# The opening of a two-block transformer kernel: the first two tiles of x as transfers and splits of their own

## What is computed

```
D_MODEL = 1024; BATCH = 1; SEQ = 256
def first_block(x, p, norm_mix_pre, w_in, ...):
    h = rms_norm(x, norm_mix_pre[l])
    z = jnp.einsum('bsd,dn->bsn', h, w_in[l])
    zq, zf_f, zf_b, zi, zg, zu, zv, ga, gb = jnp.split(z, offsets, axis=-1)
    a_out = hgrn2_mixer(...)                 # recurrent mixer on zq, zf, zi, zg
    b_out = spatial_gating(zu, zv, ...)      # gMLP unit
    merged = sigmoid(ga) * (a_out @ w_a) + sigmoid(gb) * (b_out @ w_b)
    x = x + rms_norm(merged @ w_out, norm_mix_post[l])
    ...                                      # feed-forward and a gated addition of p
def second_block(...):                       # attention, feed-forward with relu squared
    ...
def reference(...):
    return second_block(first_block(x, ...), ...)
```

## Time and profile before

| | us |
|---|---|
| median of 3 runs (804.22 to 804.37) | 804.32 |
| span of the profiled execution | 804.2 |
| that execution's whole time | 805.98 |
| PE busy in the span | 797.6 (99%) |
| ACT, DVE, POOL busy | 465.2, 571.0, 109.4 |

### The profile page before, as it was taken

How to read it: one execution, slowest core, us unless ns; L and a number is a source line. 1 busy time by engine, 2 the same in 40 slices (tenths; PEclk the granted TensorE clock), 3 DMA queues, 4 the chain that set the end, 5 groups by cost and what they waited for, 6 DMA issues and landing times.

```text
span 804.2 us, 13648 instructions
## 1 busy us (share of the span) xinstructions
PE 797.6 (99%) x5836; PEld 700.6 (87%) x5836; DVE 571.0 (71%) x713; ACT 465.2 (58%) x614; POOL 109.4 (14%) x82
## 2 busy tenths in 40 slices
PE   8999999999999999999999999999999999999998
PEld 7999988888888898888888889988899888888886
DVE  5877896796576587666676688688978865656653
ACT  6679784665534575454454575387787644444442
POOL 0101691662100000000000010111610100000000
PEclk9999999999999999999999999999999999999999
DMA  8744444453554555555555555456423555555541
GB/s 307 284 171 172 159 158 158 143 172 112 204 176 151 218 184 180 209 174 192 205 170 200 198 170 206 168 211 162 137 89 110 199 180 187 209 175 192 210 156 53
DMA packets 37820, 143.03 MB, mean 178 GB/s; under 512 B 9426, under 2 KB 11490, under 8 KB 24320
## 3 DMA queue, kind: packets, MB, share of 16 engines
q1 hardware_dynamic: 36576, 138.69, 49.7%
q0 software_dynamic: 1040, 3.43, 1.3%
q10 hardware_dynamic: 144, 0.04, 0.0%
HBM read 141.08 MB, written 1.06 MB: 177 GB/s over the span
## 4 chain that ended last, share of the span: by engine, by line
PE 96%; ACT 2%; DMA 2%; DVE 1%; issue 0%; POOL 0%; SPq 0%
PE ps L2392 8%; PE ps L2385 7%; PE ps L2032 6%; PE ps L2284 6%; PE ps L2285 6%; PE ps L2286 6%; PE ps L1964 6%; PE ps L2038 6%; PE ps L2035 6%; PE ps L1965 6%; PE ps L1966 6%; PE ps L2390 4%; PE ps L2387 4%; DMA raw<-w 2%; PE ps L2140 1%; PE ps L2300 1%
## 5 line engine op out<-in xcount | busy, mean ns | idle before, releaser
L1182 DVE TENSOR_TENSOR wlo<-raw,whi 128x2048 fp32r<-128x2048 f32 (+2 forms) x128 | 289.4, 2263 | 76.3 <-ACT whi L626 74.9
L626 ACT ACTIVATE whi<-raw 128x2048 fp32r<-128x2048 f32 (+2 forms) x128 | 241.3, 1888 | 105.6 <-DMA raw<-w 105.6
L1964 PE MATMUL ps<-xx,whi 128*128 128x256 f32 x396 | 114.1, 288 | 0.0
L1965 PE MATMUL ps<-xx,whi 128*128 128x256 f32 x396 | 112.0, 283 | 0.0
L1966 PE MATMUL ps<-xx,wlo 128*128 128x256 f32 x396 | 112.0, 283 | 0.0
L2284 PE MATMUL ps<-whi,xx 128*128 128x512 f32 x216 | 84.1, 389 | 0.0
L2285 PE MATMUL ps<-whi,xx 128*128 128x512 f32 x216 | 84.0, 389 | 0.0
L2286 PE MATMUL ps<-wlo,xx 128*128 128x512 f32 x216 | 84.0, 389 | 0.0
L2032 PE MATMUL ps<-whi,xx 128*128 128x512 f32 x208 | 83.0, 399 | 0.0
L2038 PE MATMUL ps<-wlo,xx 128*128 128x512 f32 x208 | 81.1, 390 | 0.0
L2035 PE MATMUL ps<-whi,xx 128*128 128x512 f32 x208 | 81.0, 390 | 0.0
(11 more groups left out here) (324 smaller groups left out, 1367.6 us busy)
## 6 DMA issues: line engine op xcount, KB each, us to landing
raw<-w SPq DMA_DIRECT2D x105, 1024.0 KB, 4.8
raw<-w SPq DMA_DIRECT2D x42, 512.0 KB, 5.0
raw<-w SPq DMA_DIRECT2D x8, 256.0 KB, 6.3
x<-xT SPq DMA_DIRECT2D x4, 256.0 KB, 5.7
work<-bias_scratch POOLq DMA_DIRECT2D x1, 1024.0 KB, 7.8
raw<-w SPq DMA_DIRECT2D x4, 192.0 KB, 3.3
out<-x SPq DMA_DIRECT2D x3, 256.0 KB, 2.5
raw<-w SPq DMA_DIRECT2D x3, 240.0 KB, 3.3
```

What stands on the lines that cost most here:

```text
L626: A(hi, full, ACT.Copy).then_inc(sem("hi_ready"), 1)
L1182: V.tensor_tensor(lo, full, hi.bitcast(F32), ALU.subtract)\
L1964: mm(out, hi, xh[:, tile, :], start=start, stop=False, skip_group_check=skip)
L1965: mm(out, hi, xl[:, tile, :], start=False, stop=False, skip_group_check=skip)
```

## The change

The first pair of x tiles is taken apart. SP issues x tile 0 (128 KB, `x_in0`), piece 0, x tile 1 (128 KB, `x_tile1`), piece 1, and goes on as before. ACT and DVE split tile 0, piece 0, tile 1, piece 1, each tile with its own wait and its own signal, where the two tiles stood together ahead of the two pieces. So the stage `n1` has five signals `act_hi` and `act_lo` and not four, and the waits of PE and of `gained_lo` count accordingly. The semaphores `b_hi` and `p_hi` become one, `side_hi`, and `b_lo` and `p_lo` become `side_lo`; the second user waits for 2.

```diff
-    "hi": dict(n1=4, a=4, m=4, n3=4, ff=4, n5=4, c=4, n6=4),
-    "lo": dict(n1=4, a=4, m=4, n3=4, ff=4, n5=4, c=4, n6=4),
+    "hi": dict(n1=5, a=4, m=4, n3=4, ff=4, n5=4, c=4, n6=4),
+    "lo": dict(n1=5, a=4, m=4, n3=4, ff=4, n5=4, c=4, n6=4),
...
             for k, pieces in enumerate(PIECES):
-                sp.dma_start(x[:, 2 * k:2 * k + 2, :], xT[:, 2 * k:2 * k + 2, :]).then_inc(sem(f"x_in{k}"), 16)
+                if k:
+                    sp.dma_start(x[:, 2 * k:2 * k + 2, :], xT[:, 2 * k:2 * k + 2, :]).then_inc(sem(f"x_in{k}"), 16)
                 for i in pieces:
+                    if k == 0:
+                        sp.dma_start(x[:, i, :], xT[:, i, :]).then_inc(sem(("x_in0", "x_tile1")[i]), 16)
                     u, cols = first_piece(i)
...
-            pool.wait_ge(sem("p_lo"), 1)
+            pool.wait_ge(sem("side_lo"), 2)
...
             for k, pieces in enumerate(PIECES):
-                act.wait_ge(sem(f"x_in{k}"), 16)
-                gained_hi("n1", "mix_pre", 0, k)
+                if k:
+                    act.wait_ge(sem(f"x_in{k}"), 16)
+                    gained_hi("n1", "mix_pre", 0, k)
                 for i in pieces:
+                    if k == 0:
+                        act.wait_ge(sem(("x_in0", "x_tile1")[i]), 16)
+                        A(xh[:, i, :], x[:, i, :], ACT.Copy, scale=col("mix_pre", i)).then_inc(sem("act_hi"), 1)
                     first_hi(i)
...
-                dve.wait_ge(sem("act_hi"), before("hi", name) + k + 1)
+                dve.wait_ge(sem("act_hi"), before("hi", name) + k + (2 if name == "n1" else 1))
...
+            def first_x_lo(i):
+
+                dve.wait_ge(sem(("x_in0", "x_tile1")[i]), 16)
+                dve.wait_ge(sem("act_hi"), i + 1)
+                V.scalar_tensor_tensor(xl[:, i, :], x[:, i, :], col("mix_pre", i), xh[:, i, :].bitcast(F32), ALU.mult, ALU.subtract)\
+                    .then_inc(sem("act_lo"), 1)
...
-                pe.wait_ge(sem("act_hi"), i // 2 + 1)
+                arrivals = i // 2 + 2 if i else 1
+                pe.wait_ge(sem("act_hi"), arrivals)
...
-                pe.wait_ge(sem("act_lo"), i // 2 + 1)
+                pe.wait_ge(sem("act_lo"), arrivals)
```

More of the change, by code:

```diff
@@ L801, in _ @@
                     act.wait_ge(sem("b_out"), 1)
-                    A(xh[:, 16:20, :], bout, ACT.Copy).then_inc(sem("b_hi"), 1)
+                    A(xh[:, 16:20, :], bout, ACT.Copy).then_inc(sem("side_hi"), 1)
             heads_hi_turned(2)
@@ L830, in _ @@
             act.wait_ge(sem("p_in"), 16)
-            A(xh[:, 16:18, :], pT_s, ACT.Copy).then_inc(sem("p_hi"), 1)
+            A(xh[:, 16:18, :], pT_s, ACT.Copy).then_inc(sem("side_hi"), 1)
             ahead(U_WOUT)
@@ L1250, in first_sum @@
                 link(V.tensor_tensor(sq1[:, 0:2, :], sq1[:, 0:2, :], sq1[:, 2 * k:2 * k + 2, :], ALU.add))
+            def first_x_lo(i):
[3 more added lines that the diff above has]
+                    .then_inc(sem("act_lo"), 1)
             for k, pieces in enumerate(PIECES):
-                dve.wait_ge(sem(f"x_in{k}"), 16)
-                gained_lo("n1", "mix_pre", 0, k)
+                if k:
+                    dve.wait_ge(sem(f"x_in{k}"), 16)
+                    gained_lo("n1", "mix_pre", 0, k)
                 for i in pieces:
+                    if k == 0:
+                        first_x_lo(i)
                     first_lo(i)
@@ L1420, in _ @@
                 if u == 7:
-                    dve.wait_ge(sem("b_hi"), 1)
-                    V.tensor_tensor(xl[:, 16:20, :], bout, xh[:, 16:20, :].bitcast(F32), ALU.subtract).then_inc(sem("b_lo"), 1)
+                    dve.wait_ge(sem("side_hi"), 1)
+                    V.tensor_tensor(xl[:, 16:20, :], bout, xh[:, 16:20, :].bitcast(F32), ALU.subtract).then_inc(sem("side_lo"), 1)
             def merged_lo(j):
@@ L1486, in tile_residual @@
                                        x[:, m, :], ALU.mult, ALU.add).then_inc(sem(name + "_x"), 1)
-            dve.wait_ge(sem("p_hi"), 1)
-            V.tensor_tensor(xl[:, 16:18, :], pT_s, xh[:, 16:18, :].bitcast(F32), ALU.subtract).then_inc(sem("p_lo"), 1)
+            dve.wait_ge(sem("side_hi"), 2)
+            V.tensor_tensor(xl[:, 16:18, :], pT_s, xh[:, 16:18, :].bitcast(F32), ALU.subtract).then_inc(sem("side_lo"), 1)
             V.memset(rel_s[0:33, 0, 0:HEADS], 1.0).then_inc(sem("rel_one"), 1)
@@ L2246, in _ @@
             heads_turned(1)
-            pe.wait_ge(sem("b_lo"), 1)
+            pe.wait_ge(sem("side_lo"), 1)
             bank_free(U_WB, B_BANKS[0][0])
@@ L2342, in _ @@
             arrived(U_PLE)
-            pe.wait_ge(sem("p_lo"), 1)
+            pe.wait_ge(sem("side_lo"), 2)
             ple_part(range(3))
```

## The result

The changed kernel takes 806.13 us (median of 21 runs, 805.60 to 806.88) where the kernel before takes 804.46 us on the same chip (median of 21, 804.19 to 805.37): a ratio of 1.0017, 95% interval 1.0011 to 1.0023. It is slower by 1.7 us between the two medians and by 1.4 us by the ratio (1.0017 of 804.46), outside the predicted range of 803.6 to 805.3. A few executions of several kernels took far longer (867 to 4479 us) and are left out of every ratio.

The account below looks back on a forecast made before the run. The prediction took the opening to be bound by the landing of piece 5, with PE waiting 1.16 us. Start 0 plus landings 0.1 plus 0 made +0.1 on the median 804.32: 804.4 us, range 803.6 to 805.3.

Parts of the forecast that it names:

- The base: Whole kernel: took the profiled span of 804.2 as 0.1 below the median of 804.32, and added the change to that median.
- PE has 1.16 us of slack against it: Opening, PE ahead of piece 5: supply ends last (13.72), so a sooner start only lengthens PE's 1.16 us wait.
- The start: PE's first product: from 6.19 to about 5.8, 0.4 to 0.5 us won at 7.7, but worth 0.0 at the end.
- Rival D: Opening: piece 0 lands no earlier and the start stays at 6.1; same time as forecast, counted in its 0.52 chance.
- the gains at 4.56 are untouched: ACT's start on x: the gains still land at 4.56, so tile 0 can't start sooner, however early it lands.
- covered, by 0.3 us: Piece 1 in the opening: lands at 6.1 to 6.3, high part at about 6.9, PE wants it at 7.2.
- The landings, +0.1 (bounds 0 and 0.93): Landings of piece 5, last x and unit 3: 128 more descriptors cost 0.1 us, between 0 and a whole transfer's place.
- With six transfers ahead of it this also changes nothing: Piece 5's issue on SP: shifts to between 5.0 and 5.45, but the queue ahead leaves its landing unchanged.
- C: DMA queue: the extra transfer pushes every later landing by 0.93 us, giving 805.2; chance 0.18.
- B: Landings of piece 5, last x and unit 3: issue up to 0.37 us earlier brings supply earlier, 803.9 or 803.7; chance 0.25.
- Its aside: PE's wait at 14.53: a shorter wait without the profiler would give the same time as supply coming earlier, within chance 0.25.
- The signs that were named: Opening trace: first product near 5.8, idle ahead of piece 5 about 1.45, its product 14.5 to 14.7, unit 3's high part 21.3 to 21.5.

Follow-up runs that it names:

- The hold: Changed kernel with SP holding piece 5 until piece 1 has landed: 804.52 us against 804.79 for the kernel before (0.9998); repeated on another chip, 804.58 (0.9997).
- after again: Changed kernel once more without edit, for a second trace: 806.16 us against 804.79 for the kernel before, ratio 1.0012.
- wait for tile 1: Changed kernel with one more wait on SP ahead of piece 5, for x tile 1: 805.77 us against 804.79 for the kernel before, ratio 1.0014.
- both tiles first: Changed kernel with x tiles 0 and 1 as two 128 KB transfers, both ahead of piece 0: 805.06 us against 804.88 for the kernel before, 1.0002.
- splits alone: Changed kernel with SP's part back to one 256 KB transfer for x tiles 0 and 1: 804.53 us against 804.61 for the kernel before, 0.9999.

## Why the prediction was wrong, point by point

**The base.** "A span of 804.2 that stands 0.1 below the median of 804.32" is the step that failed first. A span was compared with a whole time. Whole time to whole time, the profiled execution had taken 805.98, 1.7 us more than the median, and the table ahead of the prediction has both numbers. The usual span is 802.5 (804.32 - 1.8). So that profile was 1.7 us longer than a usual execution, and 1.0 to 1.7 us of it lay just where the argument rested, between the wait for piece 5 and the start of unit 3 (25.46 against 23.81 to 24.50).

**"PE has 1.16 us of slack against it."** In the three traces of usual length there is no such slack: PE ran from its first product (6.22, 6.64 and 6.71) to unit 2 without a gap. What the change did to the landings was not to be set against a wait that stood there anyway; it made one.

**The start.** Right, and better than forecast in its first part. PE's first product was expected near 5.8 and came at 5.78 and 5.34. Against the 6.15 to 6.71 of the seven traces with the transfers of before that is 0.4 to 1.4 us. Rival D, that piece 0 would land no earlier, is thereby out. One premise failed in the kernel's favour: "the gains at 4.56 are untouched", but they landed at 3.84 and 3.75, and ACT began tile 0 at 3.77 in the second trace. But piece 1 took most of it back: expected at 6.1 to 6.3 and "covered, by 0.3 us", it landed at 6.64 and 6.93, and PE waited 0.77 ahead of it in the second trace.

**The landings, +0.1 (bounds 0 and 0.93).** The term that was mis-sized. With the transfers of before, piece 5 landed at 11.87, 12.36 and 12.85 in the three traces of usual length, in the changed kernel at 13.33 and 13.41; unit 3 at 19.19, 19.74 and 20.32, and then at 20.80 and 21.15. That is 1.0 us at piece 5 and 1.2 at unit 3 between the means (13.37 - 12.36 and 20.98 - 19.75), above the upper bound, and the whole effect of 1.7 us, of which the traces show 1.1, is above it too. The term was sized by rows and bytes on sixteen equal engines. By bytes nothing had changed, and the quickest engine kept to that; the slowest did not.

**"With six transfers ahead of it this also changes nothing."** Wrong as a step. The depth of the queue had been taken as a cover, for the issue time of piece 5 and for all behind it. The hold shows that a queue with transfers ahead is no cover: issued 2.1 us later, piece 5 landed 2.4 us sooner, and the kernel gained 1.6 us on *after again*. That the change's own shift of this issue (to 4.96) cost anything is not shown: moved back to 5.70 by *wait for tile 1*, piece 5 still landed at 13.49.

**The rivals.** C had the direction (slower, by a landing that comes late) and said 805.2; it took too little, and its mechanism, a place in the queue for every transfer, doesn't hold, as *both tiles first* has the same number of transfers and is at 1.0002 (0.9992 to 1.0012). B (supply comes earlier with an earlier issue) falls with the two kernels that issue piece 5 of before at 4.7: 1.0005 and 1.0002. Its aside, that the wait might be shorter in a run without the profiler, isn't it either: other kernels' profiled executions lie on both sides of their medians (804.37 and 804.53, 804.89 and 804.59). That rows of 1 KB cost the time by themselves isn't it either, for they are in *both tiles first* too.

**The signs that were named.** The start near 5.8 was seen, unit 3's high part was forecast at 21.3 to 21.5 and stood at 20.82 and 21.17, and the first product of piece 5 at 14.5 to 14.7 stood at 14.13 and 14.21. PE's idle time ahead of piece 5 was to grow to 1.45; it was 0.10 and 0.30. That it would be gone had been named as a sign that the prediction is wrong. Read against the profile ahead of the prediction, the changed kernel looks no slower, and the span of before is even 0.4 us the longer one (804.2 against 803.8). The 1.7 us are found only against a usual execution of before.

**What stays open.** Shown: the loss is in SP's part, and a hold ahead of piece 5 takes it away, twice. The landings of pieces 5 to 7 from the slower DMA engines carry the part of it that the traces show (1.1 of 1.7 us), but *both tiles first* has landings as late, 13.13 and 20.50, without the timed loss. Not shown: where the rest of the 1.7 us is; why tile 1 as a transfer between pieces 0 and 1 has this effect and two tiles ahead of piece 0 have less of it; why the hold doesn't help that version; and whether a full path is the cause or only a condition, since the same early issue in the kernel before cost 0.4 to 0.5 us within intervals that hold 1. Whether rows of 1 KB are part of it was not taken apart on SP's queue. Nor was it seen which DMA engines were behind.

## What to carry to other kernels

Before a profile's waits enter a sum, set the profiled execution's whole time against the median of the runs: if it is off by more than the effect in question, its waits may not be the kernel's. In an opening that is bound by landings, ask of a reordered transfer not only whose bytes are ahead of it but also what else is under way when it goes out. Issues of 0.7 us and more on SP instead of 0.43 are a reason to try a hold, not a proof: they were there in kernels with the loss and without it (1.01 in *splits alone*). A piece that is needed late may be worth holding back behind an early landing: one wait was worth 1.6 us in the changed kernel, and nothing that could be told in before or in *both tiles first*.

## What the runs showed of the hardware that was not expected

- A transfer of 256 KB issued at 4.96 landed at 13.41, and issued at 7.08 at 11.01, in kernels that differ in that one wait.
- The sixteen parts of one transfer landed up to 4.1 us apart (9.62 to 13.73), and the last alone counts.
- With 128 KB as the first transfer instead of 256, piece 0, issued at 1.18 in both, landed at 4.50 to 4.75 in seven traces and not at 4.97 to 5.91 as in seven with the transfers of before: 0.8 us sooner between the means, where half of 1.07 us was forecast. The gains, on ACT's queue, landed at 3.64 to 4.14 and not at 4.00 to 4.62.
- The executions of the kernel before ranged from 804.0 to 806.7 us. The 0.9 us between its two profiled ones (804.2 and 803.3 of span) lie ahead of unit 3, to which PE came at 25.46 and 24.50.
